# Two of 256 row gathers, each issued as a gather of two lines and a gather of 126

## The chip, the cores and the metric

The kernel runs on one core of one Trainium2 chip. The metric is the device time of one execution in microseconds, the median of several. The kernel before took 836.07 us (three runs, 835.77 to 837.85).

## The reference, cut to what matters

One layer of a hybrid backbone is run for two groups of 128 tokens (a context pass over `x_prompt` and a denoising step over `x_sample`). State-space and attention parts come first; the last and longest part is a mixture of 16,384 tiny experts. For each token, eight heads choose 16 experts each, so 128 experts in all; of each chosen expert one line of `u_table` and one line of `v_table` are read:

```python
def one_block(args):
    xb, ib, gb = args
    act = jax.nn.gelu(jnp.einsum('nd,nhkd->nhk', xb, u_table[ib]).astype(F32)) * gb
    return jnp.einsum('nhk,nhkd->nd', act.astype(xb.dtype), v_table[ib])
...
x = x + g2 * peer(h2, p['w_query'], p['sub_keys'], p['u_table'], p['v_table'])
```

After it the result is normalised over its 1024 columns and stored. All data are fp32; `d` is 1024, `n` 128 tokens per group, `h` times `k` 128 experts.

## The kernel before, in words

The host lays the two tables side by side: `uv_table` has 16,384 lines of 2048 numbers (8 KB), the expert's u and then its v. The kernel works by *picks*: 2 groups times 128 picks make 256, numbered 0 to 255 (`LAST`); the diff's title calls them rows. Pick `p` is one expert for each of the 128 tokens of its group. A token sits on a partition, so a pick's gather brings 128 lines, one to each partition, into a page of 128 x 2048 numbers: 1 MB.

- GpSimd (POOL), `gather(pick)` (from L1522): waits until the pick's expert numbers are known (`idx_ready`, counted in fours), until the page that it will fill is free (`row_free`, which PE counts, or `row_added`, which DVE counts), and issues one indirect DMA (L1541) that reads `idx[:, pick]` and lets the 128 lines land. Each DMA counts 16 on the page's own semaphore `row_landed`. The pick `LAST` is fetched as two half rows, u first. There are 13 pages (`row_plan`), taken in turn, so a gather can be issued at most 13 picks ahead of the pick that is being finished. Between gathers POOL also does three small normalisations; one comes right after gather 160 and waits for the sum of squares of the finished prompt group (`sqf_ready`; L1448, L1449).
- VectorE (DVE), `product(pick)` (L1903): waits for the pick's row to have landed, multiplies the u half by the token's activation and sums it. Between the products it searches for the experts of later picks, in units of 32 picks (`search(u, at_)`); the expert numbers of picks 176 to 191 come out of `number(...)` (L1868 to L1878) in the step that follows product 148. After product 151 it finishes the prompt group (L1925 to L1929).
- ScalarE (ACT): gelu of the sum, times the gate (L1242, L1247), then a diagonal matrix of the 128 weights (L1253).
- TensorE (PE), `accumulate(pick)` (L866): two 128x128 by 128x512 products of that diagonal with the v half, summed in PSUM over the 128 picks of a group; then it counts the page free.
- SyncE (SP) issues plain loads in a written order. In the second half it has only these left: `final_norm` (L484), the store of `y_prompt` (L486), which waits for pick 179's place in DVE's order, and the store of `y_sample` (L489).

The order in which DVE does everything is written out by hand in one loop over the picks; POOL, ACT and PE go through the picks in order. The scratch for the descriptors of the gathers is 4096 bytes (`RING`).

The functions that the change touches:

Of the kernel before, what the change touches and what calls it, by code (L numbers as in the profile page):

```python
# [12 lines left out]
U32 = mybir.dt.uint32  # L13
# [4 lines left out]
P = 128  # L18
# [21 lines left out]
BATCH = 4  # L40
# [26 lines left out]
BY_TANH = [28, 29, 30, 31]  # L67
LAST = PICKS * G - 1
CUBE, ROOT = 0.044715, math.sqrt(2.0 / math.pi)
FIRST_SEARCH = [15, 16, 17, 18, 20, 21, 22, 24, 25, 27]  # L70
SEARCH = {2: (54, 1), 3: (77, 2)} | {u: (32 * u - 30, 2) for u in range(4, 8)}


def row_plan():
    free = [SPARE, 15, 3, 4, 5, 2, 13]
    arriving = {11: 0, 45: 15, 54: 6, 55: 7, 89: 1, 90: 14, 97: 8}
    rows, before, uses, queue = [], [], [], [(p, None) for p in free]
    count = {}
    for pick in range(PICKS * G):
        if pick in arriving:  # L80
            queue.insert(0, (arriving[pick], None))
        page_, prior = queue.pop(0)
        rows.append(page_)
        before.append(prior)
        count[page_] = count.get(page_, 0) + 1
        uses.append(count[page_])
        if pick - 2 in ADDED:
            queue.append((rows[pick - 2], pick - 2))
        if pick not in ADDED and (page_ != 15 or pick >= 45):
            queue.append((page_, pick))  # L90
    return rows, before, uses
# [44 lines left out]
def layer(nc, x_prompt, x_sample, consts_in, powers_in, w_mod01, w_mod2, b_mod, w_in_u, w_in_qkv, bmat, cmat,  # L136
# [5 lines left out]
    with ExitStack() as ctx:  # L142
        def sb(name, shape, dt=F32):
            return ctx.enter_context(nc.sbuf_tensor(name, shape, dt))

        def sem(name):
            return ctx.enter_context(nc.semaphore(name))
# [23 lines left out]
        half_neg = sb("half_neg", [P, 4])  # L171
        half_pi = sb("half_pi", [P, 1])
        consts = sb("consts", [P, sum(n for _, n in CONSTS)])
        small = sb("small", [P, 821])
        psum = ctx.enter_context(nc.psum_tensor("psum", [P, 8, 512], F32))

        cut, at = {}, 0
# [13 lines left out]
        def part(n):  # L191
            o[0] += n
            return small[:, o[0] - n:o[0]]
# [12 lines left out]
        idx = part(PICKS * G).bitcast(U32)  # L206
        gate = part(PICKS * G)
        first_idx = part(1).bitcast(U32)
        last_idx = part(2).bitcast(U32)
        inner, half_dot = part(1), part(1)  # L210
        o = [12 * PAGE + DEEP * P]
# [101 lines left out]
        def row_of(pick):  # L313
            return page(ROW[pick])
# [34 lines left out]
            sem(n) for n in ("dots_ready", "gel_ready", "wts_ready", "diag_ready", "row_free", "row_added"))  # L349
        sqf_ready, rstdf_ready, y_out_ready, stored = sem("sqf_ready"), sem("rstdf_ready"), sem("y_out_ready"), sem("stored")  # L350
        ckv_stored, ssm_stored = sem("ckv_stored"), sem("ssm_stored")
        low_summed, low_squared, low_normed, low_out = sem("low_summed"), sem("low_squared"), sem("low_normed"), sem("low_out")
        last_u_landed, last_idx_ready = sem("last_u_landed"), sem("last_idx_ready")
        ms_low = msx[:, 0:1]
# [45 lines left out]
        @block.sync  # L400
        def _(sp):
            def wait_used(name):
                if name in MOD:
                    sp.wait_ge(mod_used, MOD.index(name) + 1)
                else:
                    wait_filled(sp, LAST_USE[name])

            def load(name):
                n, at_ = ORDER[name], page_at(name)
                prior = [p for p, where in PAGES[:n] if where == at_]  # L410
                if prior:
                    wait_used(prior[-1])
                src = SRC[name]
                sp.dma_start(page(at_)[:, 0:src.shape[1]], src).then_inc(landed[at_], 16)

            def inputs_to_chunks(c):
                wait_emptied(sp, f"u_{c}")
                for j in range(4):
                    sp.dma_start(ut[:, c, j, :], us[32 * j:32 * j + 32, :, c, :]).then_inc(ut_in[c], 16)

            def kernel_windows(c):
                wait_emptied(sp, "K")
                for j in range(4):
                    rows = kern[32 * j:32 * j + 32, c, :]
                    windows = bass.AP(rows.tensor, rows.offset, [list(rows.ap[0]), [SP_, STEP], [1, STEP * SP_]])
                    sp.dma_start(toep[:, c, j, :], windows).then_inc(toep_in[c], 16)

            sp.dma_start(consts[:, :], consts_in).then_inc(consts_here, 16)
            sp.dma_start(powers.rearrange("p a k -> p (a k)"), powers_in).then_inc(powers_in_, 16)
            sp.dma_start(bm.rearrange("p r a q -> p (r a q)"), bmat).then_inc(b_in, 16)  # L430
            for k in range(2):
                load(f"mod0.{k}")
            sp.dma_start(x[:, 0, :], x_prompt).then_inc(x_in, 16)
            sp.dma_start(x[:, 1, :], x_sample).then_inc(x_in, 16)
            for k in range(2, 6):
                load(f"mod0.{k}")
            sp.wait_ge(pool_set, 1)
            sp.dma_start(brow[0:12, :], b_mod).then_inc(brow_in, 16)
            load("mod0.6")
            load("mod0.7")  # L440
            sp.dma_start(cm.rearrange("p r a q -> p (r a q)"), cmat).then_inc(c_in, 16)
            load("in_u.0")
            load("in_u.1")
            sp.dma_start(krope[:, 1, :], cache_krope).then_inc(late_in, 16)
            wait_filled(sp, "xT_0_1")
            sp.dma_start(kvb, kv_norm.to_broadcast([P, KVR])).then_inc(kvb_in, 16)
            for name in ("qkv.0", "qkv.1", "qkv.2", "mod1.0"):
                load(name)
            for c in range(3):
                inputs_to_chunks(c)  # L450
            sp.wait_ge(coef_used, 1)
            load("uq")
            sp.dma_start(page(0)[:, 1344:1728], w_uq[:, 1920:2304]).then_inc(uq_tail_in, 16)
            load("ukv")
            inputs_to_chunks(3)
            for n in range(ORDER["mod1.1"], ORDER["mod1.4"]):
                load(PAGES[n][0])
            for c in range(NC):
                kernel_windows(c)
                load(f"mod1.{4 + c}")  # L460
            load("glu")
            load("out0.1")
            sp.wait_ge(last_ready, 2 * NC)
            load("mod2a.0")
            sp.wait_ge(y_ready, 2)
            load("out1.1")
            load("out0.0")
            sp.wait_ge(y_ready, NC)
            for n in range(ORDER["mod2a.1"], ORDER["mod2b.0"]):
                load(PAGES[n][0])  # L470
            sp.dma_start(page(10), keys).then_inc(keys_in, 16)
            wait_filled(sp, "at0")
            sp.dma_start(att[1].ckvn[:, 0, :], cache_ckv).then_inc(cache_in, 16)
            load("mod2b.0")
            load("mod2b.1")
            load("query1.0")
            load("mod2b.2")
            sp.wait_ge(sq2_ready, 1)
            load("query1.1")
            load("mod2b.3")  # L480
            for n in range(ORDER["query2.0"], len(PAGES)):
                load(PAGES[n][0])
            sp.wait_ge(best_ready, 8)
            sp.dma_start(fnb, final_norm.to_broadcast([P, D])).then_inc(fn_in, 16)  # L484
            sp.wait_ge(y_out_ready, 1)
            sp.dma_start(y_prompt, h[:, 0, :]).then_inc(stored, 16)  # L486
            sp.wait_ge(low_out, 1)
            sp.wait_ge(y_out_ready, 2)
            sp.dma_start(y_sample, h[:, 1, :]).then_inc(stored, 16)  # L489
            sp.wait_ge(stored, 2 * 16)  # L490
            sp.wait_ge(ckv_stored, 2 * 16)
            sp.wait_ge(ssm_stored, 16)
# [932 lines left out]
        def _(pool):  # L1425
# [96 lines left out]
            def gather(pick):  # L1522
# [10 lines left out]
                if pick == LAST:  # L1533
                    halves_of_rows = uv_table.rearrange("n (s d) -> (n s) d", s=2)
                    pool.wait_ge(last_idx_ready, 2)
                    pool.indirect_dma_start(row_of(pick)[:, 0:D], None, halves_of_rows,
                                            bass.IndirectOffsetOnAxis(ap=last_idx[:, 0:1], axis=0)).then_inc(last_u_landed, 16)
                    pool.indirect_dma_start(row_of(pick)[:, D:2 * D], None, halves_of_rows,
                                            bass.IndirectOffsetOnAxis(ap=last_idx[:, 1:2], axis=0)).then_inc(row_landed[ROW[pick]], 16)
                    return  # L1540
                pool.indirect_dma_start(row_of(pick), None, uv_table,  # L1541
                                        bass.IndirectOffsetOnAxis(ap=idx[:, pick:pick + 1] if pick else first_idx, axis=0)).then_inc(row_landed[ROW[pick]], 16)

# [608 lines left out]
```

## Time and profile before

| what | value |
|---|---|
| median of the runs | 836.07 us |
| the profiled execution, its own time | 836.73 us |
| its span in the trace | 834.9 us |
| granted TensorE clock, mean | 0.985 |
| bytes read from HBM | 318.77 MB |
| of these through the gathers (queue q0) | 268.45 MB |
| instructions | 10350 |

The times of rows are microseconds from the span's start. The profiled execution took 836.73 us by the same clock as the runs, 1.8 us more than its span and 0.66 us more than the median. A *landing* is the moment at which a transfer's semaphore has its full count. A row can only be used when all 16 DMA engines that carry its lines have counted.

### The profile page before, as it was taken

To read this page: it belongs to the slowest core of one execution; us is meant where nothing else is said; L and a number is where in the kernel's file an instruction comes from. 1 tells how busy PE (TensorE), PEld (TensorE's weight loads), DVE (VectorE), ACT (ScalarE), POOL (GpSimd) and SP (SyncE) were. 2 spreads that over 40 slices of the span, in tenths; PEclk is the share of its full clock that TensorE was granted. 3 is DMA by queue.
4 is the path that set the end of the run, shared out by engine and by line. 5 is a ranking of instruction groups with operands and counts; after the bars stand their busy time and mean duration, and the time that the engine had idled before them with its cause. 6 is when DMAs were issued, how large, how long until landed. Compare 5 with 4: busy or idle time off the path is not lost.

```text
span 834.9 us, 10350 instructions
## 1 busy us (share of the span) xinstructions
PE 705.2 (84%) x3383; PEld 350.7 (42%) x3383; DVE 592.5 (71%) x1289; ACT 336.1 (40%) x998; POOL 380.5 (46%) x337
## 2 busy tenths in 40 slices
PE   3899999999988998899869787778777877777875
PEld 0586665656443465577524222223222222222221
DVE  7979623686995659958898756777687478744545
ACT  3423351345557333434344433343334333433332
POOL 3628900254435452445545554535544444545410
PEclk9999999999999999999999999998999999999999
DMA  9956697889999999999999999999999999999993
GB/s 372 401 204 233 219 370 273 349 304 416 413 424 362 423 422 397 420 421 423 422 420 424 422 421 423 422 421 423 421 423 423 422 423 423 422 422 423 422 423 123
DMA packets 50414, 321.74 MB, mean 385 GB/s; under 512 B 9964, under 2 KB 10668, under 8 KB 12472
## 3 DMA queue, kind: packets, MB, share of 16 engines
q0 software_dynamic: 37008, 268.45, 77.9%
q1 hardware_dynamic: 12984, 52.44, 16.2%
q8 instruction: 27, 0.44, 0.2%
q10 hardware_dynamic: 368, 0.18, 0.1%
q14 instruction: 27, 0.22, 0.1%
HBM read 318.77 MB, written 1.23 MB: 383 GB/s over the span
## 4 chain that ended last, share of the span: by engine, by line
DMA 35%; DVE 7%; PE 4%; issue 2%; ACT 2%; POOL 1%; POOLq 0%; ACTq 0%; DVEq 0%
DMA mem<-uv_table,small 35%; PE psum L866 4%; DVE mem L1903 3%; POOL mem L1541 1%; ACT mem L1253 1%; DVE modrow L1916 0%; ACT small L1247 0%; DVE mem L1853 0%; DVE x L1582 0%; DVE mem L1850 0%; ACT small L1242 0%; DVE mem L1873 0%; DVE mem L1875 0%; DVE mem L1876 0%; POOL small L1449 0%
## 5 line engine op out<-in xcount | busy, mean ns | idle before, releaser
L866 PE MATMUL psum<-mem 128*128 128x512 f32 x862 | 423.5, 621 | 98.8 <-ACT mem L1253 98.5
L1541 POOL DMA_INDIRECT mem<-uv_table,small x231 | 278.2, 1204 | 291.4 <-PE psum L866 240.6
L1903 DVE CUSTOM_DVE_ANT_0 mem<-mem,h 128x1024 f32<-128x1024 f32 x232 | 282.6, 1225 | 152.8 <-DMA mem<-uv_table,small 147.8
L866 PEld LDWEIGHTS psum<-mem 128*128 128x128 f32 x862 | 152.9, 193 | 339.1 <-ACT mem L1253 215.1
L1242 ACT ACTIVATE small<-small 128x1 f32<-128x1 f32 x252 | 50.9, 202 | 288.7 <-DVE small L1903 285.7
L1253 ACT ACTIVATE mem<-consts,small 128x128 f32<-128x128 f32 x238 | 95.6, 402 | 7.9
L1247 ACT ACTIVATE small<-small 128x1 f32<-128x1 f32 x256 | 75.4, 294 | 26.3 <-DVEq L1888 3.0
L1541 POOL DMA_INDIRECT spare_page<-uv_table,small x24 | 29.2, 1218 | 38.4 <-PE psum L866 19.4
L866 PE MATMUL psum<-spare_page,mem 128*128 128x512 f32 x88 | 42.4, 604 | 4.5 <-ACT mem L1253 4.4
L1903 DVE CUSTOM_DVE_ANT_0 spare_page<-spare_page,h 128x1024 f32<-128x1024 f32 x24 | 29.5, 1230 | 14.9 <-DMA spare_page<-uv_table,small 14.2
L799 PEld LDWEIGHTS psum<-hT,mem 128*128 128x128 f32 x288 | 34.1, 192 | 5.7 <-issue 5.7
L799 PE MATMUL psum<-hT,mem 128*128 128x128 f32 x288 | 34.3, 275 | 0.0
L521 PE MATMUL psum<-mem,scol 128*32 128x512 f32 x128 | 21.9, 771 | 14.1 <-DMA mem<-w_mod 14.1
L1448 POOL TENSOR_SCALAR small<-small 128x1 f32<-128x1 f32 (+1 forms) x8 | 6.4, 800 | 56.7 <-DVE small L1786 35.5
L866 PEld LDWEIGHTS psum<-spare_page,mem 128*128 128x128 f32 x88 | 15.6, 190 | 26.6 <-issue 14.1
L1916 DVE SCALAR_TENSOR_TENSOR modrow<-mem,small,modrow 128x1024 f32<-128x1024 f32 x15 | 19.3, 1284 | 5.4 <-ACT small L1247 5.4
L1853 DVE FIND_INDEX8 mem<-mem 128x8 uint32<-128x128 f32 (+1 forms) x64 | 22.1, 352 | 0.0
L770 PE MATMUL psum<-mem,hT 128*128 128x512 f32 x48 | 21.8, 596 | 0.3 <-PE psum L547 0.3
L1850 DVE MAX8 mem<-mem 128x8 f32<-128x128 f32 (+1 forms) x64 | 21.2, 353 | 0.2
L1057 ACT COPY late<-psum 128x512 f32<-128x512 f32 (+3 forms) x24 | 13.0, 559 | 20.2 <-PE psum L845 8.0
L1903 DVE DVE_READ_ACCUMULATOR2_ANT small<- 128x1 f32 x256 | 21.0, 82 | 0.0
L1057 ACT COPY mem<-psum 128x512 f32<-128x512 f32 (+2 forms) x26 | 14.2, 583 | 16.1 <-PE psum L583 6.2
(256 smaller groups left out, 744.1 us busy)
## 6 DMA issues: line engine op xcount, KB each, us to landing
mem<-w_mod SPq DMA_DIRECT2D x24, 1024.0 KB, 9.0
mem<-w_query SPq DMA_DIRECT2D x6, 1024.0 KB, 9.2
mem<-w_out SPq DMA_DIRECT2D x4, 1024.0 KB, 7.4
mem<-uv_table,small POOLq DMA_INDIRECT x233, 26.1
mem<-w_in_u SPq DMA_DIRECT2D x2, 1024.0 KB, 14.3
late<-w_query SPq DMA_DIRECT2D x2, 1024.0 KB, 9.4
mem<-w_in_qkv SPq DMA_DIRECT2D x2, 1008.0 KB, 12.4
mem<-w_ukv SPq DMA_DIRECT2D x1, 1024.0 KB, 8.2
```

The costliest lines, as they stand in the source:

```text
L521: mm = pe.matmul(out[32 * j:32 * j + 32, :], scol[:, k, :], w[:, j, :], start=k == 0, stop=k == KD - 1, tile_position=(0, 32 * j))
L770: mm = pe.matmul(out, mixed, weight(f"out{half}.{k // 4}", 512, 4)[:, k % 4, :], start=first and i == 0, stop=last and i == len(ks) - 1)
L799: mm = pe.matmul(bank(name)[:, P * i:P * i + P], weight(m, 512, 4)[:, k % 4, P * i:P * i + P], hT[:, k, P * g:P * g + P], start=k == 0, st ...
L866: mm = pe.matmul(bank(f"acc_{g}_{half}"), diag[:, pick % DEEP, :], row_of(pick)[:, D + 512 * half:D + 512 * half + 512], start=first, stop ...
L1057: empties(act.copy(dst, src), name)
L1242: act.activation(gel[:, cut_], dots[:, cut_], ACT.Gelu_apprx_tanh).then_inc(gel_ready, 1)
L1247: act.activation(wts[:, cut_], gel[:, cut_], ACT.Copy, scale=gate[:, pick:pick + 1]).then_inc(wts_ready, 1)
L1253: act.activation(diag[:, slot, :], ident, ACT.Copy, scale=wts[:, cut_]).then_inc(diag_ready, 1)
L1541: pool.indirect_dma_start(row_of(pick), None, uv_table, bass.IndirectOffsetOnAxis(ap=idx[:, pick:pick + 1] if pick else first_idx, axis=0) ...
L1850: last = dve.max(out_v[:, r, first_:first_ + 8], row)
L1853: last = dve.max_index(out_i[:, r, first_:first_ + 8], out_v[:, r, first_:first_ + 8], row)
L1903: dve.tensor_tensor_reduce(out=row[:, 0:D], in0=row[:, 0:D], in1=h[:, pick // PICKS, :], scale=1.0, scalar=0.0, op0=ALU.mult, op1=ALU.add, ...
```

## The change

Picks 156 and 180 are each fetched by two indirect DMAs in place of one. The first brings the lines of the last two partitions (126 and 127), the second those of partitions 0 to 125. Both count 16 on the page's semaphore, and `row_plan` counts the page's uses accordingly, so that product and `accumulate` wait for both. The indirect DMA of the two lines reads its two expert numbers from a small new tile `end_idx` on partitions 0 and 1; SP copies them there, by two small DMAs after `final_norm`'s load, each once the pick's numbers are known: for pick 156 that is idx_ready 40, for pick 180 idx_ready 46. POOL waits before gather 156 (and again before 180) until both copies have landed.

```diff
+SPLIT = [156, 180]
...
-        count[page_] = count.get(page_, 0) + 1
+        count[page_] = count.get(page_, 0) + 1 + (pick in SPLIT)
...
-        small = sb("small", [P, 821])
+        small = sb("small", [P, 829])
...
+        end_idx = part(8).bitcast(U32)
...
+        end_idx_in = sem("end_idx_in")
...
             sp.dma_start(fnb, final_norm.to_broadcast([P, D])).then_inc(fn_in, 16)
+            for at_, pick in enumerate(SPLIT):
+                sp.wait_ge(idx_ready, pick // BATCH + 1)
+                sp.dma_start(end_idx[0:2, at_:at_ + 1], idx[P - 2:P, pick:pick + 1]).then_inc(end_idx_in, 16)
             sp.wait_ge(y_out_ready, 1)
...
+                if pick in SPLIT:
+                    at_ = SPLIT.index(pick)
+                    pool.wait_ge(end_idx_in, 16 * len(SPLIT))
+                    pool.indirect_dma_start(row_of(pick)[P - 2:P, :], None, uv_table,
+                                            bass.IndirectOffsetOnAxis(ap=end_idx[0:2, at_:at_ + 1], axis=0)).then_inc(row_landed[ROW[pick]], 16)
+                    pool.indirect_dma_start(row_of(pick)[0:P - 2, :], None, uv_table,
+                                            bass.IndirectOffsetOnAxis(ap=idx[0:P - 2, pick:pick + 1], axis=0)).then_inc(row_landed[ROW[pick]], 16)
+                    return
```

## Rows read from the trace of the kernel before

**Rows 1.** The page: engines' busy time, DMA per fortieth of the span, queues.

```profile
PE 705.2 (84%) x3383; PEld 350.7 (42%) x3383; DVE 592.5 (71%) x1289; ACT 336.1 (40%) x998; POOL 380.5 (46%) x337
DMA  9956697889999999999999999999999999999993
q0 software_dynamic: 37008, 268.45, 77.9%
q14 instruction: 27, 0.22, 0.1%
```

**Rows 2.** The page: the chain that ended last, shares of the span by engine.

```profile
DMA 35%; DVE 7%; PE 4%; issue 2%; ACT 2%; POOL 1%; POOLq 0%; ACTq 0%; DVEq 0%
```

**Rows 3.** Stretches of the gather phase: busy us of each engine, PEclk, DMA share, GB/s.

```profile
450.00:550.00 100.00, 80.15 (x168) 28.71 (x167) 72.77 (x182) 40.51 (x127) 49.78 (x41) 1.00 1.01 422
660.00:800.00 140.00, 109.21 (x224) 37.94 (x223) 84.87 (x184) 53.10 (x171) 69.53 (x57) 1.00 1.01 422
```

**Rows 4.** The last 11 us of transfers in stretches of 1 us: PEclk, DMA share, GB/s.

```profile
813.50:814.50 1.00, 1.00 1.01 422
...
816.50:817.50 1.00, 1.00 0.89 365
817.50:818.50 1.00, 1.00 0.69 283
818.50:819.50 1.00, 1.00 0.44 180
819.50:820.50 1.00, 1.00 0.23 94
820.50:821.50 1.00, 1.00 0.12 49
821.50:822.50 1.00, 1.00 0.13 53
822.50:823.50 1.00, 1.00 0.08 33
823.50:824.50 1.00, 1.00 0.01 4
```

**Rows 5.** VectorE's timeline at the end, and two products earlier with a long gap.

```profile
821.78 1.23 DVE L1903 CUSTOM_DVE_ANT_0 mem<-mem,h 128x1024 f32<-128x1024 f32 x1 [1.23 <-DMA mem<-uv_table,small]
...
824.35 0.69 DVE L1582 TENSOR_TENSOR mem<-mem,late 128x512 f32<-128x512 f32 x1
...
599.52 1.23 DVE L1903 CUSTOM_DVE_ANT_0 mem<-mem,h 128x1024 f32<-128x1024 f32 x1 [0.75 <-DMA mem<-uv_table,small]
...
603.07 1.23 DVE L1903 CUSTOM_DVE_ANT_0 mem<-mem,h 128x1024 f32<-128x1024 f32 x1 [1.06 <-DMA mem<-uv_table,small]
```

**Rows 6.** DMA queues in the window 600 to 603 us.

```profile
q0 software_dynamic: 172, 1.25, 100.9%
q14 instruction: 1, 0.01, 0.7%
```

**Rows 7.** VectorE around the expert numbers of picks 176 to 191.

```profile
554.81 1.22 DVE L1903 CUSTOM_DVE_ANT_0 mem<-mem,h 128x1024 f32<-128x1024 f32 x1 [1.25 <-DMA mem<-uv_table,small]
...
558.76 0.18 DVE L1878 SCALAR_TENSOR_TENSOR small<-mem 128x16 uint32<-128x16 f32 x1
```

**Rows 8.** POOL's timeline: gathers 155, 156, 160, the normalisation, gathers 161 and 162.

```profile
544.57 0.95 POOL L1541 DMA_INDIRECT mem<-uv_table,small  x1 [1.50 <-PE psum L866]
548.07 1.45 POOL L1541 DMA_INDIRECT mem<-uv_table,small  x1 [2.56 <-PE psum L866]
...
557.43 1.40 POOL L1541 DMA_INDIRECT mem<-uv_table,small  x1 [2.03 <-PE psum L866]
569.10 1.22 POOL L1448 TENSOR_SCALAR small<-small 128x1 f32<-128x1 f32 x1 [10.27 <-DVE small L1929]
...
572.03 1.43 POOL L1541 DMA_INDIRECT mem<-uv_table,small  x1 [0.19 <-issue]
573.76 0.94 POOL L1541 DMA_INDIRECT mem<-uv_table,small  x1 [0.31 <-issue]
```

**Rows 9.** The gathers' line L1541: time from issue to landing.

```profile
DMA to landing us min/median/max: 5.5/25.9/28.9
```

**Rows 10.** DMA issues in three windows: plain transfers, KB each, us to landing.

```profile
y_prompt<-h SPq DMA_DIRECT2D x1, 512.0 KB, 7.6
...
mem<-w_query SPq DMA_DIRECT2D x2, 1024.0 KB, 9.2
...
y_sample<-h SPq DMA_DIRECT2D x1, 512.0 KB, 2.6
```

## The prediction

> **What bounds the kernel now.** I read the page first, then the chain of waits, then stretches of the gather phase, and last the final microseconds in fine stretches. The page shows no engine saturated (PE 84%, DVE 71%) but the DMA line at 9 from a third of the span on, with the gathers' queue q0 holding 77.9% of all 16 DMA engines' time [rows 1]. The chain that ended last is 35% DMA, five times the next engine [rows 2]. In 450 to 550 and in 660 to 800 us the DMA share is 1.01 at 422 GB/s [rows 3]: the phase runs at the pace of the transfers. One row is 1,048,576 bytes, at 422 GB/s 2.485 us. q0 has 37,008 packets for 257 gathers, 144 each, so 9 for each of 16 engines: 8 lines of 8 KB and one count [rows 1]. One line is thus 2.485 / 8 = 0.311 us of one engine.
>
> What the totals hide is that the 16 engines don't finish together. At 813.5 to 814.5 all are busy (1.01). From 816.5 the share falls: 0.89, 0.69, 0.44, 0.23, 0.12, 0.13, 0.08, 0.01 [rows 4]. Times 16 that is 14, 11, 7.0, 3.7, 1.9, 2.1, 1.3 and 0.2 engines. So from 820.5 to 822.5 just two engines still work; one stops at about 822.8 (1.3 engine-us are left in that stretch, one of them the last engine's), the other at about 823.66. DVE's last wait on a transfer ends with them: the v half of the last row is used at 824.35 [rows 5]. The other 14 are done by 820.4 (of 3.7 engine-us in 819.5 to 820.5 two are the laggards', 1.7 belong to engines that stop in it). The rate of the others doesn't rise when engines stop (two engines, 49 to 53 GB/s, 26 each, as 422 / 16 = 26.4) [rows 4]: each engine has its own limit, and what one is behind it doesn't make up. The laggards lose time in steps. Product 167 starts at 603.07, 3.55 us after the one before, against 2.485 in the steady state [rows 5], and in that window q14 has one instruction packet, all other packets being gathers' [rows 6]. There are 27 such packets [rows 1], and I take it that the same engines serve them each time, since two are so far behind at the end.
>
> **The change, part by part.**
>
> *Work moved between engines.* How a gather of 2 or of 126 lines is dealt out no row shows. Bounds by the nearest row (128 lines, 8 on each of 16 engines): either the lines stay as evenly spread as they can (126 over 16 engines, 8 at most on any), or they go in equal shares, and 126 = 14 x 9 leaves two engines free, which have the two lines of the first gather. I take equal shares, because 128 is dealt exactly equally. Per split, 14 engines then carry 9 lines in place of 8 (+0.31 us) and a pair carries 1 in place of 8 (7 x 0.311 = 2.17 us less); for two splits, if the pair is the same, +0.62 and -4.35.
>
> [...]
>
> *If the pair is the two laggards* the ends move thus: 823.66 - 4.35 = 819.3; 822.8 - 4.35 = 818.5; the other 14: 820.4 + 0.62 = 821.0. The last engine ends 823.66 - 821.0 = 2.65 us earlier. All that follows (10.5 us from 824.35 to the span's end at 834.9) hangs on that landing and moves with it. Steps that come after pick 180 are already in the end times. So -2.65, which is my value; the ends of this term are +0.62 (the pair is two others) and -2.65.
>
> *POOL's issue.* Two more indirect DMAs, 0.95 to 1.45 us with 0.3 between [rows 8], some 2.5 us of an engine that is busy half the time (49.8 of 100) [rows 3] and works with 25.9 us (median) between issue and landing [rows 9]. Hidden: 0. Without that cover it would be 2.5.
>
> *The new wait at gather 156.* It was issued at 548.07 [rows 8]. Now it waits for the copy that needs pick 180's numbers, which DVE writes at 558.76 + 0.18 = 558.94 [rows 7]. Behind it on POOL stand gathers 157 to 160, the normalisation and 161. SP has nothing else to do then. How long does the tiny copy take? Beside gathers, 512 KB took 7.6 us and 1024 KB 9.2, so zero bytes would take about 6.0; alone, 512 KB took 2.6 [rows 10]. Bounds 2.6 and 9.2, taken 6.0, nearest to rows under the same load. Then: landed 565.1; two-line gather from 565.4, 0.95, gap 0.3, the 126-line gather at 566.7; lines start to flow at most 5.5 - 2.5 = 3.0 us later [rows 9]: 569.7. When do the engines run dry? Product 148 began at 554.81 upon its landing [rows 7]; row 155, the last one issued (544.57 [rows 8]), is seven later: 554.81 + 17.4 = 572.2 on the last engine. The engine that is third at the end is 3.3 before the last one there; had it been so here it is dry at 568.9 and stands 0.8 us; since the laggard got at least one step of 1.07 later (603.07 [rows 5]) the third was nearer then, dry after 569.9, and stands not at all. Faster engines stand longer, up to 4 us, but have that much to give. Cost 0; bounds 0 and, with a copy of 9.2 us, 4.0. The followers catch up: POOL issues one in 1.25 us, the engines eat one in 2.485. 157 to 160 end at about 573; 161 comes at about 576.5 instead of 572.03, and its row is needed by the fastest engine only at 569.7 + 5 x 2.485 = 582.1. The normalisation's result is read some 18 picks later.
>
> *At 180* both numbers are long there; only the issue counts. *SP's y_prompt store* is not due until pick 179, 31 picks after the new copy before it.
>
> *Sum*: -2.65 + 0 + 0. Against the profiled execution's own 836.73 that is 834.1; its difference to the median of the runs is 0.66, so 836.07 - 2.65 = 833.4.
>
> **The rivals.**
>
> *The pair is not the two laggards.* Both end 0.62 later: 836.7, slower, though hardly by what can be measured. [...]
>
> [...]
>
> *An even spread.* 126 lines put 8 on 15 engines and 6 on the last; it saves 2 x 2 x 0.311 = 1.24 us, the first two engines get 0.62. If the last engine is the last laggard: 823.66 - 1.24 = 822.4, the other laggard at 822.8 decides, gain 0.9: 835.2. If not, 0 or +0.6. For it: 128 lines can't tell it from equal shares.
>
> *The wait decides.* With the copy late by more than about 6.2 us the third engine stands one for one. At 9.2 us it is 3 to 4: if the pair is right the gain is gone (836.6), if it is wrong the laggard too is held from 572.2 on, and every later row with it. The same price could come from the 126-line gather if its lines, nine to an engine, go slower than eight: 2 x 2.8 us at half pace. Taken together a case at 839, slower; for it, POOL's own wait of 10.27 us before 569.10 already drains the queue there (161 is issued 15 us after 160) [rows 8]; against, that wait costs nothing now, DVE's spacing stays 2.485.
>
> *Relieved, but partly eaten* by either of these: 835.
>
> **How the numbers follow.** The two laggards relieved, nearly in full: 0.48. Even spread: 0.14. Wrong pair: 0.20. Partly eaten: 0.06. The wait or slow lines decide: 0.12. This kernel can tell about 0.3% (2.5 us) from no change, so the limit is 833.56. The first case lies just beyond it: of its 0.48 I put 0.38 beyond and 0.10 within. Faster 0.38; slower 0.12; same 0.10 + 0.14 + 0.20 + 0.06 = 0.50. The likeliest case's own range is 832.5 to 834.8. The range for all reaches to the wrong pair and a little of the last case: 832.5 to 837.6.
>
> **What the profile after would show.** The final stretches: where the share now has a shelf of two engines for 3 us, it falls to zero within about 4 us of its start. A shelf of the same length, later by 0.6, means the wrong pair; one a little shorter, the even spread. At 565 POOL's gather of two lines after a wait of about 14 us; DMA share below 1 around 569 for fast engines only. DVE's waits on product 156 and 157 would show whether the wait reached the last engine: more than 2.5 us between their starts is against me. The prediction is wrong if the end of transfers moves by less than 2 us.

## The result: slower by 9 us, and the profile after

The changed kernel took 845.63 us (four runs, 845.03 to 845.88), the kernel before 836.48 us beside it. The ratio is 1.0105, interval 1.0093 to 1.0117: 9 us slower. I had forecast 833.4 and a range of 832.5 to 837.6.

The stretches of the changed kernel, in the columns of [rows 3]:

```profile
450.00:550.00 100.00, 79.80 (x167) 28.77 (x166) 71.83 (x177) 40.49 (x126) 46.67 (x39) 1.00 1.01 422
560.00:580.00 20.00, 15.94 (x28) 6.34 (x28) 13.83 (x24) 6.17 (x21) 12.70 (x13) 0.83 0.99 340
580.00:625.00 45.00, 33.47 (x69) 11.62 (x69) 31.39 (x81) 16.17 (x54) 24.30 (x22) 1.00 1.01 422
625.00:645.00 20.00, 14.88 (x28) 5.16 (x28) 12.05 (x31) 5.39 (x18) 7.92 (x7) 0.91 1.01 331
660.00:800.00 140.00, 110.51 (x223) 38.92 (x224) 85.59 (x185) 52.48 (x169) 67.82 (x57) 0.99 1.01 422
```

Before, between and after the two split rows the rate is 422 GB/s, as in [rows 3]. In the two stretches in which the split rows are carried it is 340 and 331. The lost bytes are 20 x (422 - 340) / 422 = 3.9 us and 20 x 91 / 422 = 4.3 us, together 8.2 of the 9. Beside the rate stands the DMA share, and it stays at 0.99 and 1.01. By the share the engines are not waiting for work, they are slow. In the worst window of the first stretch, 570 to 575 us:

```profile
DMA packets 178, 1.22 MB, mean 244 GB/s; under 512 B 29, under 2 KB 29, under 8 KB 29
q0 software_dynamic: 178, 1.22, 100.2%
```

Only 178 - 29 = 149 lines of 8 KB pass in 16 x 5 = 80 us of engine time: 0.54 us a line, against 0.311 before. POOL's timeline, whose first row answers to [rows 8], and SP's second copy:

```profile
544.05 0.95 POOL L1555 DMA_INDIRECT mem<-uv_table,small  x1 [1.65 <-PE psum L872]
564.22 0.89 POOL L1550 DMA_INDIRECT mem<-uv_table,small  x1 [19.22 <-DMA small<-small]
565.41 0.98 POOL L1552 DMA_INDIRECT mem<-uv_table,small  x1 [0.31 <-issue]
...
558.51 0.61 SPq L490 DMA_DIRECT2D small<-small  x1
```

The wait is there: POOL stands 19.2 us before the gather of two lines. The end of the transfers, in the columns of [rows 4]:

```profile
825.50:826.50 1.00, 1.00 0.41 156
826.50:827.50 1.00, 1.00 0.14 57
827.50:828.50 1.00, 1.00 0.06 25
...
831.50:832.50 1.00, 1.00 0.07 29
832.50:833.50 1.00, 1.00 0.02 8
```

Where two engines worked alone at the end of the kernel before, one does now (0.06 x 16 = 1.0), for 5 us. By these shares one of the two laggards has been relieved, the other has not, and it is further behind the rest than it was. The other 15 are done by 827.5, the last at about 832.8: over 5 us, against 3.3 before.

### The profile page after: what moved, and what is told of

Read it like the earlier page. It is cut to its first block, busy times and chain, and to the rows that moved or that the text cites. A ratio compares the mean times of both kernels' runs of the same rounds, so it can differ in the third digit from the quotient of the medians.

```text
span 844.1 us, 10354 instructions
## 1 busy us (share of the span) xinstructions
PE 713.0 (84%) x3383; PEld 353.5 (42%) x3383; DVE 592.3 (70%) x1289; ACT 336.2 (40%) x998; POOL 381.3 (45%) x339
## 4 chain that ended last, share of the span: by engine, by line
DMA 35%; DVE 7%; PE 6%; issue 2%; ACT 2%; POOL 1%; POOLq 0%; ACTq 0%; DVEq 0%
DMA mem<-uv_table,small 31%; PE psum L872 5%; DMA spare_page<-uv_table,small 3%; DVE mem L1917 3%; ACT mem L1259 1%; DMA small<-small 1%; POOL mem L1555 1%; ACT small L1253 0%; DVE modrow L1930 0%; PE psum L572 0%; DVE mem L1867 0%; DVE mem L1889 0%; DVE mem L1887 0%; DVE mem L1890 0%; DVE spare_page L1917 0%
## 5 line engine op out<-in xcount | busy, mean ns | idle before, releaser
L872 PE MATMUL psum<-mem 128*128 128x512 f32 x862 | 430.2, 630 | 100.9 <-ACT mem L1259 98.4
L872 PEld LDWEIGHTS psum<-mem 128*128 128x128 f32 x862 | 155.0, 195 | 345.4 <-ACT mem L1259 213.3
L1930 DVE SCALAR_TENSOR_TENSOR modrow<-mem,small,modrow 128x1024 f32<-128x1024 f32 x15 | 19.2, 1283 | 8.4 <-ACT small L1253 8.4
```

The source lines that it names most:

```text
L872: mm = pe.matmul(bank(f"acc_{g}_{half}"), diag[:, pick % DEEP, :], row_of(pick)[:, D + 512 * half:D + 512 * half + 512], start=first, stop ...
```

## The experiments

Times are given as ratios to the kernel before on the same chip; in us they are the ratio's excess times 837. Each run starts from the changed kernel unless it says otherwise. Lists of parts stand in the order of issue. A line or a row is called *misdealt* when it belongs to a transfer that is cut by partitions; the *skew* is the time by which the first engine is ahead of the last.

**One split alone, at 180.** `-SPLIT = [156, 180]`, `+SPLIT = [180]`.

> Pick 180 alone is split (2 + 126 lines); pick 156 is one gather again, and no gather waits for anything new near 560 us. Theory A (meeting writes: a gather that is not dealt like the 128-line one makes engines write where others write, and every line slows): half of the cost stays, 840 to 841.5 us (+4 to +5 over before), with a stretch of 10 us after 625 at about 250 GB/s instead of 422. Theory B (the wait at gather 156 emptied the queue, and what comes later is its echo): within 1 us of before, 836 to 837, no slow stretch. Theory C (only the load of 14 engines grows, by 0.31 us per split): +0.3, 836.5.

Measured 841.64, ratio 1.0057 (1.0041 to 1.0074), +4.8 us. The rate in 625 to 640:

```profile
625.00:630.00 5.00, 1.00 1.06 241
630.00:635.00 5.00, 0.88 1.00 216
635.00:640.00 5.00, 0.78 0.99 380
```

Half the cost, with no new wait near 560 and a slow stretch (241 and 216 GB/s): what theory A forecast; B and C fall. What the run shows is that the lines are slow, and where in time. No view names an engine or the place that it writes, so the meeting of writes is a supposition here and in all the runs that follow.

**The waits without the splits.** In `gather`, after the wait, the usual line for 128 lines (and in `row_plan` one use for the page, as before):

```diff
                 if pick in SPLIT:
                     at_ = SPLIT.index(pick)
                     pool.wait_ge(end_idx_in, 16 * len(SPLIT))
-                    pool.indirect_dma_start(row_of(pick)[P - 2:P, :], ...
-                    pool.indirect_dma_start(row_of(pick)[0:P - 2, :], ...
-                    return
```

> The two small copies by SP and POOL's wait for them before gathers 156 and 180 stay, but both picks are fetched by one gather of 128 lines. Theory A: the wait costs only the engines that are ahead, total within 1 us of before, 836 to 837.5. Theory B: most of the 9 us stays, 842 to 845. In both the stretch 565 to 570 falls below 422 GB/s for want of descriptors; under A the DMA share falls with it, because the engines stand and are not slow.

Measured 837.91 against 837.06, ratio 1.0001 (0.9988 to 1.0014); the medians differ by 0.85 us, which lies within that interval. POOL stands 19.20 us as in the change (the view puts the wait down to PE, but the page was free long before: without the copy this gather went out at 548.07 [rows 8]), and the rate falls a little behind it:

```profile
566.33 0.94 POOL L1550 DMA_INDIRECT mem<-uv_table,small  x1 [19.20 <-PE psum L872]
...
565.00:570.00 5.00, 0.75 0.99 395
570.00:575.00 5.00, 0.93 1.01 419
```

5 x 27 / 422 = 0.3 us of the mean engine. None of it shows on the last: VectorE's products 156 and 157 start at 576.25 and 578.68, 2.43 us apart. The wait costs nothing that these runs can tell, 1.2 us at most.

**Two gathers of 64 lines.** `SPLIT = {180: [(0, 64), (64, 128)]}`, the expert numbers of the second half copied to partitions 0 to 63.

> Pick 180 alone is fetched as two gathers of 64 lines (partitions 0 to 63, then 64 to 127), which 16 engines can share equally, 4 lines each. [...] Theory C, and theory D (a count of engines that is not 16 is what is slow): no cost, 836 to 837.

Measured 842.79, ratio 1.0066 (1.0047 to 1.0086), +5.5 us:

```profile
630.00:635.00 5.00, 1.98 (x4) 0.68 (x4) 1.89 (x5) 1.10 (x4) 2.16 (x2) 1.00 1.00 229
```

C and D fall if the lines are shared as the expectation supposes: then 16 engines with four lines each are slow too.

**Two gathers of 128 half lines.** Starting from the kernel before, for pick 180:

```diff
+                    for i in range(2):
+                        pool.indirect_dma_start(row_of(pick)[:, D * i:D * i + D], None, halves_of_rows,
+                                                bass.IndirectOffsetOnAxis(ap=two_idx[:, i:i + 1], axis=0)).then_inc(...)
```

> Pick 180 alone is fetched as two gathers of 128 half lines each (u, then v), as the last pick is already; DVE computes two index columns more. Theory A: dealt like every other gather, so no cost: 836 to 837, 422 GB/s throughout. Theory E (a second indirect DMA for one pick is itself what costs, by its issue or its count): as e1, 840 to 841.5.

Measured 835.88 against 837.06, ratio 0.9989 (0.9979 to 0.9999), with the usual rate throughout:

```profile
630.00:635.00 5.00, 1.00 1.01 420
635.00:640.00 5.00, 1.00 1.00 421
```

A second indirect DMA for a pick costs nothing that these runs can tell; E falls. Whether this version is the faster one, as the ratio's end just allows, is below what I would claim.

**Parts of 16 and 112 lines.** `SPLIT = {180: [(112, 128), (0, 112)]}`. Both parts are multiples of 16 lines, so that 16 engines could share each of them equally, 1 + 7 = 8 lines an engine. That they do is a supposition, from the eight lines an engine of a usual gather [rows 1]; theories C and D would then see no cost.

> Pick 180 alone, lines of partitions 112 to 127 first, then those of 0 to 111. [...]

Measured 842.2, ratio 1.0074 (1.0057 to 1.0091), +6.2 us. The window 630 to 635:

```profile
DMA packets 161, 1.11 MB, mean 223 GB/s; under 512 B 25, under 2 KB 25, under 8 KB 25
q0 software_dynamic: 161, 1.11, 101.5%
```

161 - 25 = 136 lines in 80 us of engine time, 0.59 us each. If the lines are shared equally, C and D fall here too, and what remains different from a usual gather is the cut by partitions itself. The trace doesn't show the sharing.

**The other order.** `SPLIT = {180: [(0, 126), (126, 128)]}`.

> Pick 180 alone, split as in the change but in the other order: 126 lines first, then the last two. Theory A: the slow stretch is the same, +4 to +5 us, 840 to 842. [...]

Measured 843.56, ratio 1.009 (1.0071 to 1.0108), +7.5 us. The shelves at the end of e1 and then of this run:

```profile
825.00:826.00 1.00, 1.00 0.06 25
826.00:827.00 1.00, 1.00 0.07 29
```

```profile
825.00:826.00 1.00, 1.00 0.14 57
826.00:827.00 1.00, 1.00 0.13 53
```

By the shares that is one engine there (0.06 x 16 = 1.0) and two here (0.13 x 16 = 2.1). So the order decides who is relieved: with the two lines first it is one of the laggards, with the 126 lines first neither. That the one relieved is the last but one, and not the last, is taken from e7 below. The expectation's range was passed by 1.6 us.

**The split at pick 254, both orders.** `SPLIT = {254: [(126, 128), (0, 126)]}`, then `{254: [(0, 126), (126, 128)]}`.

> The same split (2 lines, then 126) for pick 254 instead, the last whole row. The slow stretch then falls where most engines are about to stop, 3 to 7 us ahead of the last one. Theory A: most of the slowness is hidden in that slack; the last engine, not in the relieved pair by the trace of the change, carries 9 lines, some of them slow: +0.3 to +3.5 us, 836.5 to 840. If the cost were of the gather itself wherever it stands: 841 to 842.

> Pick 254 with the 126 lines first. If the pair that this order relieves holds the last engine: -2.2 us less what the slow lines cost it, 834 to 836. If not: as e7.

Measured 841.74, ratio 1.0069 (1.005 to 1.0089), and 841.12, ratio 1.0072 (1.0052 to 1.0092). The first was a miss: I thought that the slack of 14 engines would hide the slow lines, and the time fell where I had put a cost of the gather itself. The second came out by its other branch, "as e7": neither order relieves the last engine. VectorE's products 249 to 254 in e7 start when the last engine has carried its part:

```profile
808.46 1.22 DVE L1918 CUSTOM_DVE_ANT_0 mem<-mem,h 128x1024 f32<-128x1024 f32 x1 [1.25 <-DMA mem<-uv_table,small]
...
811.45 1.23 DVE L1918 CUSTOM_DVE_ANT_0 mem<-mem,h 128x1024 f32<-128x1024 f32 x1 [1.75 <-DMA mem<-uv_table,small]
...
816.37 1.23 DVE L1918 CUSTOM_DVE_ANT_0 mem<-mem,h 128x1024 f32<-128x1024 f32 x1 [3.69 <-DMA mem<-uv_table,small]
...
821.19 1.23 DVE L1918 CUSTOM_DVE_ANT_0 mem<-mem,h 128x1024 f32<-128x1024 f32 x1 [3.59 <-DMA mem<-uv_table,small]
...
824.09 1.23 DVE L1918 CUSTOM_DVE_ANT_0 mem<-mem,h 128x1024 f32<-128x1024 f32 x1 [1.66 <-DMA mem<-uv_table,small]
...
826.87 1.23 DVE L1918 CUSTOM_DVE_ANT_0 mem<-mem,h 128x1024 f32<-128x1024 f32 x1 [1.55 <-DMA mem<-uv_table,small]
```

Between the second, third and fourth lie 4.92 and 4.82 us instead of 2.485. These are rows 251 and 252, gathered as always and issued ahead of row 254. In 811 to 813 and 813 to 815 us the rate is 244 and 205 GB/s at a DMA share of 1.07 and 1.06, so the other engines are by then at the misdealt lines, I take it, and the last engine is slowed in its own usual ones. The slack of the others didn't protect it. Product 254 starts 2.78 us after product 253, and nine lines at 0.311 us would take 2.80: by this estimate the last engine carries nine, so it isn't the relieved one.

**Eight in a row.** `SPLIT = {p: [(112, 128), (0, 112)] for p in range(180, 188)}`.

> Picks 180 to 187, all eight as 16 + 112 lines. Theory A1 (a misdealt line is slow whatever stands beside it): 64 lines per engine at about 0.535 us instead of 0.311, +14 us, and the mixed edges once, +2 to +4: 852 to 855 us. Theory A2 (slow is only the meeting of misdealt and usual gathers on different engines at the same time): the cost is about that of one, +6 to +9, 842 to 845. Theory G (each split costs its own 6 us): +45 to +50, 882 to 887.

Measured 857.57, ratio 1.0245 (1.0226 to 1.0265), +20.5 us, 2.6 for each. In the middle of the stretch:

```profile
658.39 1.23 DVE L1918 CUSTOM_DVE_ANT_0 spare_page<-spare_page,h 128x1024 f32<-128x1024 f32 x1 [2.95 <-DMA spare_page<-uv_table,small]
663.19 1.23 DVE L1918 CUSTOM_DVE_ANT_0 mem<-mem,h 128x1024 f32<-128x1024 f32 x1 [3.57 <-DMA mem<-uv_table,small]
667.96 1.23 DVE L1918 CUSTOM_DVE_ANT_0 mem<-mem,h 128x1024 f32<-128x1024 f32 x1 [3.54 <-DMA mem<-uv_table,small]
```

4.8 us a row where 2.485 is usual, and

```profile
660.00:665.00 5.00, 1.00 1.03 215
```

Misdealt rows are slow among themselves too: about half pace (215 of 422). A2 and G fall by far; A1's kind is right, its size 2.6 us too low. Eight times 2.3 us is 18.5, and that leaves 2.0 for the mixed edges, the time in which some engines are at misdealt rows and others are not. In the single split of the same cut (e5, +6.2) the same subtraction leaves 3.9. So the edges are worth 2 to 4 us, a large part of what a single split costs; with intervals of 1.4 to 1.7 us on either side the runs don't fix the share.

**The place of one split.** `SPLIT = {112: ...}`, `{236: ...}`, `{156: ...}`, each with `[(126, 128), (0, 126)]`.

> One split (2 + 126) at pick 112, whose row is carried near 465 us, when the first and last engine are about 3 us apart (they are 6 apart at pick 180). Theory A with the stretch as its price: it lasts from the first engine's start of the misdealt lines to the last one's end, skew + 9 x 0.535 = 7.8 us, and costs 1 - 244/422 = 0.42 of it: +3.3 us, 838.5 to 840. Theory H (a fixed cost per split): +4.8 as e1, 840.5 to 842.

> The same split at pick 236, where the skew is about 7 to 8 us. Stretch as price: 12.3 us, 0.42 of it is +5.2 us, 841 to 842.5, at least 1 us over e10. Fixed cost: as e10.

> Pick 156 alone is split (2 + 126), its number is copied as soon as known, 80 us ahead, so that no gather waits for pick 180's. Stretch as price, skew about 4.5: 9.3 us x 0.42 = +3.9 us, 839 to 840.5. With e1 this must make up the change's +9. If the wait had a part in the change, e12 and e1 together fall short of it by more than 1.5 us.

Measured 841.75, ratio 1.0068 (1.0047 to 1.009), +5.7 us; 844.26, ratio 1.0085 (1.0064 to 1.0106), +7.1; 842.78, ratio 1.0069 (1.0049 to 1.0088), +5.8. All are 1.9 to 2.4 us above what I worked out for them. By its time e10 fell into theory H's range, e11 into neither. The slow stretches of e10, of e12 and then of e11:

```profile
455.00:460.00 5.00, 1.00 1.06 274
460.00:465.00 5.00, 1.00 0.98 221
465.00:470.00 5.00, 1.00 1.02 413
```

```profile
565.00:570.00 5.00, 1.00 1.04 379
570.00:575.00 5.00, 0.68 1.02 218
575.00:580.00 5.00, 0.64 0.99 321
580.00:585.00 5.00, 1.00 1.02 410
```

```profile
765.00:770.00 5.00, 1.00 1.02 311
770.00:775.00 5.00, 1.00 1.04 226
775.00:780.00 5.00, 0.66 0.98 257
780.00:785.00 5.00, 1.00 1.01 392
```

Below 422 GB/s the first loses 5 x (148 + 201 + 9) / 422 = 4.2 us, the last 5 x (111 + 196 + 165 + 30) / 422 = 5.9; between them lie e12 with 4.3 and e1, by its lines above, with 5.1. The order is that of the picks, 112, 156, 180 and 236, and so of the skew. In the traces the stretch thus grows with the skew, in one execution of each run. The times don't show it: their intervals overlap, and the trace of e10 is of its fastest execution, 838.84 us, while others took up to 843.0. A fixed cost of about 6 us per split isn't excluded by them. (In e7, e8 and e11 SP also stores y_prompt later than otherwise, because its copy of the split pick's numbers stands before it; e1, e10 and e12 have no such delay and cost 4.8 to 5.8.)

Pick 156 alone and pick 180 alone add up to 10.6 us, more than the 9.1 of both: nothing is left for the wait.

In e1, e6, e7 and e9 to e12, where the expectations give theory A's range of times, the median came out above its upper end each time, by 0.1 us in e1 and 2.6 us in e9. The kind of cost was foreseen (of its place in e7 not); its size was taken too low, and why is not shown.

**Plain loads.** Starting from the kernel before; `FN_PARTS` is `[(0, 112), (112, 128)]` in the first run and `[(0, 128)]` in its control (VectorE's waits on `fn_in` are raised to the new counts):

```diff
-            sp.dma_start(fnb, final_norm.to_broadcast([P, D])).then_inc(fn_in, 16)
+            for again in range(6):
+                for lo, hi in FN_PARTS:
+                    sp.dma_start(fnb[lo:hi, :], final_norm.to_broadcast([hi - lo, D])).then_inc(fn_in, 16)
+                sp.wait_ge(fn_in, 16 * len(FN_PARTS) * (again + 1))
```

> Gathers as before. SP's load of final_norm (512 KB, 128 partitions) is made six times in a row instead of once, each time as partitions 0 to 111 and 112 to 127, each pair waited for. If it matters where the engines write: each pair slows all engines for some us while it lands, GB/s below 400 for most of 421 to 480 us, +4 to +15 us over e14. If the slowness is of GpSimd's descriptors: as e14 within 1 us, 422 GB/s.

> The control of e13: the same six loads, each as one transfer to 128 partitions. Both theories: five more loads of 512 KB at 1.24 us each, +6.2 us over before, 842 to 844 us, at 420 GB/s all along.

Measured 852.62, ratio 1.0172 (1.0149 to 1.0195), and for the control 842.78, ratio 1.006 (1.0043 to 1.0077): 9.4 us by the ratios between loads that differ in the cut and in being twelve transfers instead of six (the control's +5.0 is near the 6.2 worked out for five more loads). The same stretch, split and then whole:

```profile
445.00:455.00 10.00, 0.83 1.02 355
```

```profile
445.00:455.00 10.00, 1.00 1.01 422
```

Over the 60 us from 425 to 485 the split run's six such stretches stand at 353, 366, 355, 349, 357 and 365 GB/s; against 422 that is 9.2 us lost, as much as the difference of the times. No gather is cut here, so the slowness is not one of the gathers' own descriptors. The usual gathers beside the plain loads that are cut by partitions are slowed with them. Two things weren't run: the plain load cut in two by columns, which would part the cut from the mere number of transfers (for gathers e4 has done that), and one part of a cut transfer without the other, which would tell which of the two is slow.

## Why the prediction was wrong, step by step

- *What bounds the kernel* held in the main: the transfers do, and two engines were last. "Each engine has its own limit" held for usual lines (the one engine that works at the end moves 25 to 29 GB/s, as 422 / 16 = 26.4); that engines can slow one another wasn't in it, and e7 has the last engine at 4.9 us a row instead of 2.485. That the two laggards are the ones that serve the instruction packets remains the guess that it was: no run tested it. Steps after the landing moved with it: the v half of the last row is used at 833.52 instead of 824.35, 9.2 us later, and the span grew by 9.2.

```profile
833.52 0.69 DVE L1596 TENSOR_TENSOR mem<-mem,late 128x512 f32<-128x512 f32 x1
```

- *Work moved between engines* is the step that failed. It gave 2 x (-2.17) to a pair and 2 x 0.31 to the rest, and all of it at 0.311 us a line. That price came from rows in which every transfer goes to 128 partitions. Cut otherwise, a line takes 0.54 to 0.59 us in the worst windows, and not only the cut gather's: the engines together run at about half pace there (216 to 244 GB/s in the change and with one split, 215 in e9). No run shows how 2 or 126 lines are shared among the engines, that the two engines left free get the two lines, or that both splits relieve the same pair; the -4.35 and the +0.62 were an estimate on that supposition. What the runs showed in their place is +4.8 us (e1) and +5.8 us (e12) for a split.
- I had the right price in view and misplaced it. The rival "the wait decides" held a clause on lines at half pace, 2 x 2.8 us, within a case of 0.12 at 839. It counted only the 14 engines' own nine lines, 5.6 us; the lines of other rows that were slowed meanwhile make up the rest of the 9. It was a mechanism of its own and should have had its own number.
- *Who is relieved*: half right. The shelf of one engine after (share 0.06), and of two with the order turned (0.13, e6), say that one laggard was relieved and the other not, and e7's 2.78 us, near nine lines' 2.80, that the other is the last engine. Even at full pace per line the last engine would by the same estimate have ended 0.6 later, not 2.65 earlier: the case that I had at 0.20.
- *The new wait*: right in its cost. 0 taken, 0.1 us measured (e2, -1.0 to +1.2); the gather of two lines at 564.22 where I had 565.4; the copy ended at most 5.7 us after its issue at 558.51, against 6.0. The wait of "about 14 us" that I named as a sign was a slip: from the end of gather 155 (544.57 + 0.95) to 565.4 my own rows give 19.9, and it was 19.2.
- *POOL's issue*: right, hidden (e4, where a second indirect DMA costs nothing).

The cause as the runs bound it: neither the wait (e2), nor a second DMA (e4), nor the gathers' descriptors (e13), nor, if lines are shared equally, an unequal load or a number of engines other than 16 (e3, e5). What the runs show is that a row cut by partitions slows everything in flight (216 to 244 GB/s in the worst windows instead of 422, at a DMA share of 0.98 to 1.04), and a row cut by columns doesn't (420 and 421 GB/s). Why that is so was not shown: no view names an engine or the place that it writes, so that the writes meet remains my supposition. Why cuts as different as 64 + 64 (229 GB/s), 16 + 112 (223) and 2 + 126 (216) all come out near half of 422 remains open as well.

## What to carry to other kernels

Where transfers bound a kernel as here, try first to let all of them span the same 128 partitions, and to make one smaller by its columns: cut so, a row left the rate at 420 and 421 GB/s (e4), cut by partitions it cost 4.8 to 7.5 us (e1, e3, e5 to e8, e10 to e12). A transfer cut by partitions slowed the transfers beside it from GpSimd's queue (216 GB/s in e1's worst window) and from SP's (349 to 366 in e13), and the last engine even in the rows issued ahead of it (e7), so the slack of the others hid nothing of it. And a per-line price read from uniform transfers (0.311 us) didn't hold for others (0.54 to 0.59 in the worst windows): when a change makes a shape that the trace lacks, price the whole stretch at half pace as a rival of its own.

## What the runs showed of the hardware that I had not expected

A plain load of 512 KB cut into 112 and 16 partitions cost 9.4 / 6 = 1.6 us more than the same load whole, beside gathers that were not touched (e13, e14). The last engine, still at rows gathered as usual, went from 2.485 to 4.9 us a row ahead of a misdealt one (e7). And a full DMA share went with 216 GB/s (e1, 630 to 635 us, share 1.00) and 244 (after the change, 570 to 575, 1.00) as well as with 422 (1.01): the share alone doesn't say that the engines move all they can.
